# Strassen products in a conv output projection: half of two column groups as seven products of half blocks

## The chip, the cores and the metric

One core of a Trainium2 chip runs the whole program. The metric is the device time of one execution in microseconds (us). The kernel before takes 827.39 us (median of three runs, 826.68 to 827.71).

## The reference

An encoder trunk of two layers on x of 256 rows by 2048 features: a gated differential-attention layer and then a gated Conformer convolution layer, each added to x, and a final RMSNorm. The change lies at the end of the convolution layer, and in it this part matters:

```python
h = xn @ w_in + b_in                          # 2048 -> 3 x 2048
a, g, z = jnp.split(h, [CONV_WIDTH, 2 * CONV_WIDTH], axis=-1)
u = a * jax.nn.sigmoid(g)
u = depthwise_conv(u, dw, 31 taps) + dw_b     # along the rows
u = silu(layernorm(u) * ln_g + ln_b)
y = (u * jax.nn.silu(z)) @ w_out + b_out      # 256 x 2048 times 2048 x 2048
x = x + y
out = rmsnorm(x) * final_gain
```

## The kernel before, in words

All arrays are fp32. TensorE multiplies in fp32r, so each operand is held as a high part (a copy rounded to fp32r) and a low part (the operand minus its high part), and every product is three matmuls: high by high, high by low, low by high.

Weights stream through a ring of four slots (`RING`). A chunk is four k-tiles (`CK`) by 512 columns (`GW`), 1 MB. SyncE's queue loads it into `w_raw[slot]`; ScalarE makes the high part `w_hi` (`high_part`, L476) once the chunk has landed and TensorE has used the chunk four before it (`w_free`); VectorE (`low_part`, L826) or GpSimd (`low_part`, L448) makes the low part `w_lo`; TensorE multiplies; SyncE reloads the raw slot when the low part is done. Each engine works strictly through its own list, whose order is written out by hand; semaphores tie the lists together.

The convolution layer's input projection is 64 chunks (`CHUNKS_OUT` to `CHUNKS_CONV`). While TensorE works on them, VectorE makes the 30 remaining taps in PSUM (L1065) and GpSimd makes the gate products (`gate`, L461) and the low parts of chunks `POOL_FROM` up to `POOL_TO`, that is up to the fourth chunk of the output projection. Then come the layer norm (L1105 to L1112, L1118), the SiLUs, `gate_block(b)` (L1127, VectorE: silu(u) times silu(z) for two k-tiles), `block_hi(b)` (L681, ScalarE) and `block_lo(b)` (L1131, VectorE), which make the left operand of the output projection.

The output projection is 16 chunks in four column groups n = 0 to 3 of 512 columns, four chunks each; they are called chunk 0 to chunk 15 here. Each chunk is 4 k-tiles by 2 row halves (`st`) by 3 matmuls of 512 columns: 24 matmuls (`project`, L1247, L1249, L1250). Group n accumulates in banks `acc[2*(n%2)+st]`, so a group's banks have a whole further group of time to be emptied. VectorE adds b_out to the rows (`with_bias`, L1163), adds the product from PSUM (`with_product`, L1171) and multiplies by the final gain (`with_gain`, L1177). ScalarE squares the sums (L785) for the final norm. Group 3 is worked row half by row half, in banks that already hold x plus b_out, so that only half of it is left to finish at the end.

## Time and profile before

| | before |
|---|---|
| median of 3 runs | 827.39 us (826.68 to 827.71) |
| the profiled execution's own time | 826.85 us |
| span in its trace | 825.1 us |
| TensorE matmul busy | 817.6 us, 99% of the span |
| VectorE busy | 645.7 us, 78% |
| ScalarE busy | 450.1 us, 55% |
| GpSimd busy | 228.8 us, 28% |
| mean granted TensorE clock | 0.999 |

The profile is of one execution. The span goes from its first to its last instruction; 1.75 us of the execution's own time lie outside it. "Busy" of TensorE is an average that hides how tightly its matmuls follow each other: the spacing of their starts says more. PE is TensorE, DVE VectorE, ACT ScalarE, POOL GpSimd, SP SyncE.

### The profile page before, as it was taken

What the parts mean: (1) busy time and instruction counts of PE and PEld (TensorE: products, weight loads), DVE (VectorE), ACT (ScalarE), POOL (GpSimd) and SP (SyncE); (2) the same over time, 40 slices, a digit from 0 to 9 for tenths busy, and PEclk for the clock granted to TensorE, in tenths of its full rate; (3) what the DMA queues carried; (4) which work ended last, traced back from release to release, by engine and by line L of the source; (5) the groups of instructions that cost most, each with busy time, mean ns of one, the idle gap of its engine ahead of it and who ended that gap; (6) DMA issues with size and microseconds to landing.
All of it is one profiled execution on the core that took longest, in us unless ns stands there. A gap on an engine that the chain in (4) does not pass through costs nothing.

```text
span 825.1 us, 13852 instructions
## 1 busy us (share of the span) xinstructions
PE 817.6 (99%) x5628; PEld 756.1 (92%) x5628; DVE 645.7 (78%) x1099; ACT 450.1 (55%) x590; POOL 228.8 (28%) x107
## 2 busy tenths in 40 slices
PE   9999999999999999999999999999999999999996
PEld 9998899889998899888888999999999999998885
DVE  7578785697659785798788988999999998656651
ACT  7756643546436643556544465465555556694432
POOL 0300000000000000002000009988989887680000
PEclk9999999999999999999999999999999999999999
DMA  9987566536654566525655666655655565549502
GB/s 330 394 290 272 173 204 216 192 122 205 227 187 146 171 212 212 189 102 173 228 175 189 204 193 215 204 175 185 204 191 175 197 203 176 185 154 355 195 10 102
DMA packets 99809, 163.68 MB, mean 198 GB/s; under 512 B 3616, under 2 KB 40992, under 8 KB 99240
## 3 DMA queue, kind: packets, MB, share of 16 engines
q1 hardware_dynamic: 98128, 160.51, 57.8%
q10 hardware_dynamic: 1624, 2.38, 0.8%
q8 instruction: 39, 0.64, 0.3%
q14 instruction: 18, 0.15, 0.1%
HBM read 160.76 MB, written 3.69 MB: 199 GB/s over the span
## 4 chain that ended last, share of the span: by engine, by line
PE 56%; DVE 38%; ACT 4%; issue 2%; POOL 0%; ACTq 0%; DVEq 0%; POOLq 0%
DVE ps_d L1065 23%; PE ps_acc L1247 9%; PE ps_acc L1249 9%; PE ps_acc L1250 9%; PE ps_acc L1263 7%; PE ps_acc L1264 7%; PE ps_acc L1261 7%; DVE sb_w_lo L826 6%; DVE sb_zT L1017 3%; ACT sb_w_hi L476 2%; PE ps_acc L1307 1%; PE ps_acc L1311 1%; PE ps_acc L1314 1%; DVE sb_mT L980 1%; DVE sb_probs L948 1%
## 5 line engine op out<-in xcount | busy, mean ns | idle before, releaser
L476 ACT ACTIVATE sb_w_hi<-sb_w_raw 128x2048 fp32r<-128x2048 f32 x139 | 265.6, 1918 | 224.4 <-PE ps_acc L1264 151.9
L448 POOL TENSOR_TENSOR sb_w_lo<-sb_w_raw,sb_w_hi 128x2048 fp32r<-128x2048 f32 x45 | 208.2, 4633 | 389.2 <-ACT sb_w_hi L476 389.2
L826 DVE TENSOR_TENSOR sb_w_lo<-sb_w_raw,sb_w_hi 128x2048 fp32r<-128x2048 f32 x94 | 213.6, 2289 | 90.8 <-ACT sb_w_hi L476 90.4
L1261 PE MATMUL ps_acc<-sb_conv_hi,sb_w_hi 128*128 128x256 f32 x768 | 213.1, 278 | 0.0
L1264 PE MATMUL ps_acc<-sb_conv_hi,sb_w_lo 128*128 128x256 f32 x768 | 212.1, 276 | 0.0
L1263 PE MATMUL ps_acc<-sb_conv_lo,sb_w_hi 128*128 128x256 f32 x768 | 212.1, 276 | 0.0
L1065 DVE SCALAR_TENSOR_TENSOR ps_d<-sb_uT,sb_dwT,ps_d 128x256 f32<-128x256 f32 x480 | 189.0, 490 | 4.5 <-ACT ps_d L707 4.5
L1247 PE MATMUL ps_acc<-sb_w_hi,sb_act_hi 128*128 128x512 f32 x384 | 149.7, 390 | 0.0
L1249 PE MATMUL ps_acc<-sb_w_lo,sb_act_hi 128*128 128x512 f32 x384 | 149.6, 390 | 0.0
L1250 PE MATMUL ps_acc<-sb_w_hi,sb_act_lo 128*128 128x512 f32 x384 | 149.4, 389 | 0.0
L1263 PEld LDWEIGHTS ps_acc<-sb_conv_lo,sb_w_hi 128*128 128x128 f32 x768 | 144.2, 188 | 0.1
L1261 PEld LDWEIGHTS ps_acc<-sb_conv_hi,sb_w_hi 128*128 128x128 f32 x768 | 144.2, 188 | 0.1
L1264 PEld LDWEIGHTS ps_acc<-sb_conv_hi,sb_w_lo 128*128 128x128 f32 x768 | 144.2, 188 | 0.0
L1261 PE MATMUL ps_acc<-sb_act_hi,sb_w_hi 128*128 128x256 f32 x448 | 123.9, 276 | 0.0
L1264 PE MATMUL ps_acc<-sb_act_hi,sb_w_lo 128*128 128x256 f32 x448 | 123.7, 276 | 0.0
L1263 PE MATMUL ps_acc<-sb_act_lo,sb_w_hi 128*128 128x256 f32 x448 | 123.7, 276 | 0.0
L1250 PEld LDWEIGHTS ps_acc<-sb_w_hi,sb_act_lo 128*128 128x128 f32 x384 | 72.1, 188 | 15.1
L1247 PEld LDWEIGHTS ps_acc<-sb_w_hi,sb_act_hi 128*128 128x128 f32 x384 | 72.1, 188 | 15.0 <-DVE sb_act_lo L999 0.4
L1249 PEld LDWEIGHTS ps_acc<-sb_w_lo,sb_act_hi 128*128 128x128 f32 x384 | 72.1, 188 | 14.2
L1261 PEld LDWEIGHTS ps_acc<-sb_act_hi,sb_w_hi 128*128 128x128 f32 x448 | 84.1, 188 | 0.1
L1263 PEld LDWEIGHTS ps_acc<-sb_act_lo,sb_w_hi 128*128 128x128 f32 x448 | 84.1, 188 | 0.1
L1264 PEld LDWEIGHTS ps_acc<-sb_act_hi,sb_w_lo 128*128 128x128 f32 x448 | 84.1, 188 | 0.0
(171 smaller groups left out, 880.4 us busy)
## 6 DMA issues: line engine op xcount, KB each, us to landing
sb_w_raw<-in_attn_w_in SPq DMA_DIRECT2D x59, 1024.0 KB, 5.8
sb_w_raw<-in_conv_w_in SPq DMA_DIRECT2D x64, 512.0 KB, 4.6
sb_w_raw<-in_attn_w_out SPq DMA_DIRECT2D x16, 1024.0 KB, 5.0
sb_w_raw<-in_conv_w_in SPq DMA_DIRECT2D x16, 1024.0 KB, 5.1
sb_w_raw<-in_conv_w_out SPq DMA_DIRECT2D x16, 1024.0 KB, 5.0
sb_w_raw<-in_attn_w_in SPq DMA_DIRECT2D x15, 256.0 KB, 4.2
sb_xs<-in_x SPq DMA_DIRECT2D x2, 1024.0 KB, 12.3
sb_x_in<-in_x_turned SPq DMA_DIRECT2D x15, 128.0 KB, 4.0
```

The costliest lines, as they stand in the source:

```text
L448: pool.tensor_tensor(w_part(w_lo, c), w_raw[c % RING][:], w_part(w_hi, c).bitcast(F32), ALU.subtract).then_inc(lo_ready_pool, 1)
L476: act.activation(w_part(w_hi, c if like is None else like), w_raw[slot][:], ACT.Copy).then_inc(hi_ready, 1)
L826: dve.tensor_tensor(w_part(w_lo, like), w_raw[slot][:], w_part(w_hi, like).bitcast(F32), ALU.subtract).then_inc(lo_ready, 1)
L948: ins = dve.transpose(probs_turned[b * Q:(b + 1) * Q, :, :, a * Q:(a + 1) * Q], src[:, b])
L1017: ins = dve.transpose(dst, src)
L1065: dve.scalar_tensor_tensor(out_, uT[:, k, tap:tap + SEQ], dwT[:, k, tap:tap + 1], out_, ALU.mult, ALU.add).then_inc(tap_done, 1)
L1247: pe.matmul(into, left_hi, high[:, k], start=(kt == 0 and not filled), stop=False, skip_group_check=filled)
L1249: pe.matmul(into, left_hi, low[:, k], start=False, stop=False, skip_group_check=filled)
L1250: ins = pe.matmul(into, left_lo, high[:, k], start=False, stop=(kt == KT - 1), skip_group_check=filled)
L1261: pe.matmul(into, left_hi, hi[:, kt], start=(kt == 0 and f % 2 == 0), stop=False, skip_group_check=True)
L1263: pe.matmul(into, left_hi, lo[:, kt], start=False, stop=False, skip_group_check=True)
L1264: ins = pe.matmul(into, left_lo, hi[:, kt], start=False, stop=(kt == KT - 1), skip_group_check=True)
```

## The change

Chunks 0 to 3 (group 0) stay, in `acc` banks 0 and 1. Groups 1 and 2 are now interleaved: chunks 4 and 5 are their first 512 rows of weights, chunks 6 and 7 the next 512. They run one row half at a time, in four banks (`OWN_BANKS`) which ScalarE fills beforehand with x plus b_out (`fill`): group 1 has banks 3 and 0, group 2 banks 2 and 1. Banks 0 and 1 are those of group 0. Chunks 8 to 11 are the other 1024 rows of groups 1 and 2; two chunks at a time (a "quarter", q) they form a 2 by 2 matrix of half blocks (2 k-tiles by 512 columns), and with the two row halves of the left operand this is a product of 2 by 2 block matrices. It is done in Winograd's form of Strassen's scheme: seven products instead of eight, each 2 k-tiles by 3 matmuls. The sums of the left blocks (`row_sums`) and of the weight blocks (`sum_of_blocks`) are VectorE's, high and low parts are made of the sums (`sum_high`, `factor_hi` on ScalarE; `sum_low`, `factor_lo` on VectorE), and VectorE combines the products. Chunks 12 to 15 are group 3 as before.

b_out is loaded early and GpSimd adds it to all of x in two instructions of 128 x 2048, in the input projection's groups 1 and 3. GpSimd's last low part is now that of chunk 1; those of chunks 2 and 3 are VectorE's. The products of gate_block 4 to 7 go to SBUF. The diff at its core (declarations, semaphores and the renamed helpers of `project` are left out, and empty lines too):

```diff
+SEVEN_AT = CHUNKS_CONV + 2 * NCH
+SEVEN_UPTO = SEVEN_AT + NCH
+QUARTERS = 2
+FIRST = NCH - QUARTERS
+B11, B21, T3, B22, T2, T4, T1 = range(7)
+FACTORS = (B11, B21, T3, B22, T2, T4, T1)
+S1, S2, S3, S4 = range(4)
 POOL_FROM = CHUNKS_OUT + 2 * RING
-POOL_TO = CHUNKS_CONV + RING
+POOL_TO = CHUNKS_CONV + 2
...
+        def raw_factor(q, f):
+            c = SEVEN_AT + 2 * q + (f in (T3, B22, T1))
+            rows = HALVES[f in (B21, B22, T4)]
+            return w_raw[c % RING][:, rows]
...
+        def factors_done(q, f):
+            return len(FACTORS) * q + f + 1
...
+        SEVEN_BANKS = {B11: bank_a[1][:], B21: acc[:, 3], T3: bank_a[0][:], B22: acc[:, 2], T2: bank_d[0][:],
+                       T4: acc[:, 0], T1: bank_d[1][:]}
+        OWN_BANKS = {(1, 0): acc[:, 3], (2, 0): acc[:, 2], (1, 1): acc[:, 0], (2, 1): acc[:, 1]}
+        FILLED = ((1, 0), (2, 0), (1, 1), (2, 1))
+        LAST_BANKS = (bank_a[1][:], acc[:, 3])
...
+                if g == 0:
+                    sp.wait_ge(ss_ready, ST + 2 * PAIRS)
+                    sp.dma_start(b_out_bc, bass.AP(conv_b_out.tensor, conv_b_out.offset, [[0, P], [1, D]])
+                                 ).then_inc(b_out_landed, 16)
+            while c < CHUNKS:
+                n, i = conv_out_chunk(c)
+                if of_seven(c - RING):
+                    sp.wait_ge(seven_lo, len(FACTORS) * ((c - RING - SEVEN_AT) // 2 + 1))
+                else:
                     low_part_ready(sp, c - RING)
-                    load(i, cw_out[:, i * CK:(i + 1) * CK, n * GW:(n + 1) * GW])
...
+                load(c % RING, cw_out[:, i * CK:(i + 1) * CK, n * GW:(n + 1) * GW])
+                c += 1
+                if c == SEVEN_UPTO:
+                    sp.wait_ge(sum_lo, 4)
+                    sp.dma_start(gain_bc, bass.AP(final_gain.tensor, final_gain.offset, [[0, P], [1, D]])
                                  ).then_inc(final_landed, 16)
...
+                if (n, f) == (1, 0):
+                    pool.wait_ge(b_out_landed, 16)
+                    pool.wait_ge(x1_turned, PAIRS)
+                if f == 0 and n in (1, 3):
+                    st = n // 2
+                    pool.tensor_tensor(xs[:, st], xs[:, st], b_out_bc, ALU.add).then_inc(biased, 1)
                 low_part(c)
...
+                    act.wait_ge(factor_ready, 4 * q + 1 + (T3, T2, T4, T1).index(f))
+                if q:
+                    act.wait_ge(seven_used, factors_done(q - 1, f))
+                else:
+                    act.wait_ge(w_free, SEVEN_AT + f // 2 + 1)
+                act.activation(factor(w_hi, f), raw_factor(q, f), ACT.Copy).then_inc(seven_hi, 1)
+            def fill(bank, n, st):
...
+                act.activation(bank, xs[:, st, n * GW:(n + 1) * GW], ACT.Copy).then_inc(bank_filled, 1)
...
+            def sum_high(i):
+                act.wait_ge(sum_ready, 4)
+                act.activation(sums_hi[:, i].rearrange("p (q k) s -> p q k s", k=2), sums_in_place()[i], ACT.Copy
+                               ).then_inc(sum_hi, 1)
             hi_of(CHUNKS_CONV + RING)
+            act.wait_ge(acc_free, scaled_by(N_CONV - 1))
+            act.wait_ge(biased, ST)
+            fill(OWN_BANKS[1, 0], 1, 0)
+            fill(OWN_BANKS[2, 0], 2, 0)
             load_table(ACT.Sqrt)
+            for i in (S3, S4, S2, S1):
+                sum_high(i)
...
+            def last_high(i):
+                act.wait_ge(landed[i], 16 * loads_of(SEVEN_UPTO + i))
+                act.wait_ge(seven_used, factors_done(QUARTERS - 1, min(2 * i + 1, T1)))
+                act.activation(w_part(w_hi, SEVEN_UPTO + i), w_raw[i][:], ACT.Copy).then_inc(hi_ready, 1)
+            hi_of(CHUNKS_CONV + RING + 1)
+            hi_of(CHUNKS_CONV + RING + 2)
+            for st in range(ST):
+                act.wait_ge(y_ready, st + 1)
+                fill(OWN_BANKS[1 + st, 1], 1 + st, 1)
+            hi_of(CHUNKS_CONV + RING + 3)
+            act.wait_ge(sum_lo, 4)
+            for st in range(ST):
+                squares_of_y(0, st)
+            for q in range(QUARTERS):
+                for f in FACTORS:
+                    factor_hi(q, f)
+            act.wait_ge(seven_used, factors_done(QUARTERS - 1, B11))
+            act.activation(partial[:, 0], SEVEN_BANKS[B11], ACT.Copy).then_inc(first_copied, 1)
+            act.wait_ge(first_copied, 1)
+            fill(LAST_BANKS[0], PAIRS - 1, 0)
+            last_high(0)
+            act.wait_ge(y_ready, 3)
+            fill(LAST_BANKS[1], PAIRS - 1, 1)
+            for i in range(1, NCH):
+                last_high(i)
+            for n in (1, 2):
+                for st in range(ST):
+                    squares_of_y(n, st)
...
+                dve.tensor_tensor(gated_tile(b), gated_bank(b), block_of(zT, b), ALU.mult).then_inc(gated, 1)
...
+            low_part(CHUNKS_CONV + 2, 2)
             block_lo(6)
             block_lo(7)
...
+            low_part(CHUNKS_CONV + 3, 3)
...
+            def factor_lo(q, f):
+                dve.wait_ge(seven_hi, factors_done(q, f))
+                dve.tensor_tensor(factor(w_lo, f), raw_factor(q, f), factor(w_hi, f).bitcast(F32), ALU.subtract
+                                  ).then_inc(seven_lo, 1)
...
+            def row_sums():
+                s = sums_in_place()
+                a11, a12, a21, a22 = s[S2], s[S4], s[S3], s[S1]
+                dve.tensor_tensor(s[S1], a21, a22, ALU.add).then_inc(sum_ready, 1)
+                dve.wait_ge(sum_ready, 1)
+                dve.tensor_tensor(s[S3], a11, a21, ALU.subtract).then_inc(sum_ready, 1)
+                dve.wait_ge(sum_ready, 2)
+                dve.tensor_tensor(s[S2], s[S1], a11, ALU.subtract).then_inc(sum_ready, 1)
+                dve.wait_ge(sum_ready, 3)
+                dve.tensor_tensor(s[S4], a12, s[S2], ALU.subtract).then_inc(sum_ready, 1)
...
+            def sum_low(n, i):
+                dve.wait_ge(sum_hi, n + 1)
+                dve.tensor_tensor(sums_lo[:, i].rearrange("p (q k) s -> p q k s", k=2), sums_in_place()[i],
+                                  sums_hi[:, i].rearrange("p (q k) s -> p q k s", k=2).bitcast(F32), ALU.subtract
+                                  ).then_inc(sum_lo, 1)
...
+            def sum_of_blocks(q, f):
+                b11, b21, b12, b22 = (raw_factor(q, g) for g in (B11, B21, T3, B22))
+                if f == T3:
+                    for c in (SEVEN_AT + 2 * q, SEVEN_AT + 2 * q + 1):
+                        dve.wait_ge(landed[c % RING], 16 * loads_of(c))
+                    dve.tensor_tensor(b12, b22, b12, ALU.subtract).then_inc(factor_ready, 1)
+                elif f == T2:
+                    dve.wait_ge(factor_ready, 4 * q + 1)
+                    dve.wait_ge(seven_lo, factors_done(q, B11))
+                    dve.tensor_tensor(b11, b12, b11, ALU.add).then_inc(factor_ready, 1)
+                elif f == T4:
+                    dve.wait_ge(factor_ready, 4 * q + 2)
+                    dve.wait_ge(seven_lo, factors_done(q, B21))
+                    dve.tensor_tensor(b21, b21, b11, ALU.subtract).then_inc(factor_ready, 1)
+                else:
+                    dve.wait_ge(seven_lo, factors_done(q, T3))
+                    dve.tensor_tensor(b12, b22, b11, ALU.subtract).then_inc(factor_ready, 1)
...
-            low_parts(0, 4)
-            dve.wait_ge(final_landed, 32)
-            for n in range(last):
-                for st in range(ST):
-                    with_bias(n, st, xs[:, st, n * GW:(n + 1) * GW])
-                if n == 0:
-                    with_product(0)
-            low_parts(4, 6)
+            low_part(CHUNKS_CONV + RING, 0)
+            dve.wait_ge(s_lo, BLOCKS)
+            row_sums()
+            low_part(CHUNKS_CONV + RING + 1, 1)
+            for n, i in enumerate((S3, S4, S2, S1)):
+                sum_low(n, i)
+            low_part(CHUNKS_CONV + RING + 2, 2)
+            dve.wait_ge(w_free, RING + CHUNKS_CONV + NCH)
+            dve.wait_ge(biased, ST)
+            for st in range(ST):
+                dve.tensor_tensor(y_of(0, st), acc[:, st], y_of(0, st), ALU.add).then_inc(y_ready, 1)
+            low_part(CHUNKS_CONV + RING + 3, 3)
+            sum_of_blocks(0, T3)
+            factor_lo(0, B11)
+            factor_lo(0, B21)
+            sum_of_blocks(0, T2)
+            sum_of_blocks(0, T4)
+            dve.wait_ge(final_landed, 16)
             with_gain(0)
...
+            factor_lo(0, T3)
+            factor_lo(0, B22)
+            sum_of_blocks(0, T1)
+            sum_of_blocks(1, T3)
+            factor_lo(0, T2)
+            factor_lo(0, T4)
+            factor_lo(0, T1)
+            factor_lo(1, B11)
+            factor_lo(1, B21)
+            sum_of_blocks(1, T2)
+            sum_of_blocks(1, T4)
+            factor_lo(1, T3)
+            factor_lo(1, B22)
+            sum_of_blocks(1, T1)
+            factor_lo(1, T2)
+            factor_lo(1, T4)
+            factor_lo(1, T1)
+            done = factors_done(QUARTERS - 1, 0)
+            dve.wait_ge(first_copied, 1)
+            dve.wait_ge(seven_used, done + B21)
+            dve.tensor_tensor(y_of(1, 0), partial[:, 0], SEVEN_BANKS[B21], ALU.add).then_inc(y_ready, 1)
+            last_low(0)
+            dve.wait_ge(seven_used, done + T2)
+            link(dve.tensor_tensor(partial[:, 0], partial[:, 0], SEVEN_BANKS[T2], ALU.add))
+            link(dve.tensor_tensor(partial[:, 1], partial[:, 0], SEVEN_BANKS[T3], ALU.add))
+            dve.wait_ge(seven_used, done + T4)
+            dve.tensor_tensor(y_of(1, 1), partial[:, 1], SEVEN_BANKS[T4], ALU.add).then_inc(y_ready, 1)
+            last_low(1)
+            last_low(2)
+            last_low(3)
+            dve.wait_ge(seven_used, done + T1)
+            link(dve.tensor_tensor(partial[:, 0], partial[:, 0], SEVEN_BANKS[T1], ALU.add))
+            dve.tensor_tensor(y_of(2, 0), partial[:, 0], SEVEN_BANKS[B22], ALU.add).then_inc(y_ready, 1)
+            dve.wait_ge(y_ready, 4)
+            link(dve.tensor_tensor(partial[:, 1], partial[:, 1], SEVEN_BANKS[T1], ALU.add))
+            dve.tensor_tensor(y_of(2, 1), partial[:, 1], OWN_BANKS[2, 1], ALU.add).then_inc(y_ready, 1)
             with_gain(1)
...
+            for i in range(NCH):
+                c = CHUNKS_CONV + i
                 low_part_ready(pe, c)
-                if i < NCH:
-                    pe.wait_ge(s_lo, 2 * i + 1)
-                if i % NCH == 0:
-                    if n < 2:
-                        pe.wait_ge(acc_free, 2 * (G_CONV_IN + N_CONV + n + 1))
-                    else:
-                        pe.wait_ge(y_ready, 2 * (n - 1))
-                project(c, i % NCH, n % 2, conv_hi, conv_lo,
-                        (lambda: pe.wait_ge(s_lo, 2 * i + 2)) if i < NCH else None)
-            pe.wait_ge(y_ready_pre, 2 * PAIRS)
+                pe.wait_ge(s_lo, 2 * i + 1)
+                if i == 0:
+                    pe.wait_ge(acc_free, scaled_by(N_CONV - 2))
+                project(c, i, 0, conv_hi, conv_lo, lambda: pe.wait_ge(s_lo, 2 * i + 2))
...
+            for c in range(CHUNKS_CONV + NCH, SEVEN_AT):
+                n, i = conv_out_chunk(c)
+                low_part_ready(pe, c)
+                for st in range(ST):
+                    if i == 0:
+                        pe.wait_ge(bank_filled, FILLED.index((n, st)) + 1)
+                    project(c, i, 0, conv_hi, conv_lo, tiles=(st,), done=w_free if st else None,
+                            filled={st: OWN_BANKS[n, st]})
+            for q in range(QUARTERS):
+                for f in FACTORS:
+                    pe.wait_ge(seven_lo, factors_done(q, f))
+                    if q == 0:
+                        pe.wait_ge(gated, BLOCKS)
+                        if f in (T3, B22, T2, T1):
+                            pe.wait_ge(sum_lo, (T3, B22, T2, T1).index(f) + 1)
+                    into, high, low = SEVEN_BANKS[f], factor(w_hi, f), factor(w_lo, f)
+                    on = f in (B21, B22, T4)
+                    for k in range(2):
+                        left_hi, left_lo = left_tiles(q, f, k)
+                        end = q == QUARTERS - 1 and k == 1
+                        pe.matmul(into, left_hi, high[:, k], start=(q == 0 and k == 0 and not on), stop=False,
+                                  skip_group_check=on)
+                        pe.matmul(into, left_hi, low[:, k], start=False, stop=False, skip_group_check=on)
+                        ins = pe.matmul(into, left_lo, high[:, k], start=False, stop=end, skip_group_check=on)
+                    ins.then_inc(seven_used, 1)
             for st in range(ST):
+                pe.wait_ge(bank_filled, len(FILLED) + st + 1)
                 for i in range(NCH):
                     if st == 0:
                         low_part_ready(pe, CHUNKS - NCH + i)
                     project(CHUNKS - NCH + i, i, (PAIRS - 1) % 2, conv_hi, conv_lo, tiles=(st,),
-                            done=rows_done if i == NCH - 1 else None, filled=True)
```

## Rows read from the trace of the kernel before

**Rows 1.** The page: busy us, share of the span and instructions.
```profile
PE 817.6 (99%) x5628; PEld 756.1 (92%) x5628; DVE 645.7 (78%) x1099; ACT 450.1 (55%) x590; POOL 228.8 (28%) x107
```
**Rows 2.** Waits, TensorE's only one: us in total, times, longest us.
```profile
PE ps_d L1364 <- POOL sb_ones L426: 1.0, 1, 1.0
```
**Rows 3.** Timeline of TensorE, output projection: start us, us, instruction.
```profile
731.47 0.40 PE L1247 MATMUL ps_acc<-sb_w_hi,sb_conv_hi 128*128 128x512 f32 x1
...
753.26 0.39 PE L1247 MATMUL ps_acc<-sb_w_hi,sb_conv_hi 128*128 128x512 f32 x1
...
755.98 0.39 PE L1247 MATMUL ps_acc<-sb_w_hi,sb_conv_hi 128*128 128x512 f32 x1
...
818.31 0.39 PE L1250 MATMUL ps_acc<-sb_w_hi,sb_conv_lo 128*128 128x512 f32 x1
```
**Rows 4.** Timeline of VectorE, 737 to 803 us; idle before it in brackets.
```profile
738.33 0.70 DVE L1127 TENSOR_TENSOR ps_d<-ps_d,sb_zT 128x512 f32<-128x512 f32 x1
738.94 0.68 DVE L1131 TENSOR_TENSOR sb_conv_lo<-ps_a,sb_conv_hi 128x512 fp32r<-128x512 f32 x1
...
755.47 2.29 DVE L826 TENSOR_TENSOR sb_w_lo<-sb_w_raw,sb_w_hi 128x2048 fp32r<-128x2048 f32 x1 [3.15 <-ACT sb_w_hi L476]
757.68 1.29 DVE L1163 TENSOR_TENSOR sb_xs<-sb_xs,sb_b_out_bc 128x512 f32<-128x512 f32 x2
758.88 1.28 DVE L1171 TENSOR_TENSOR sb_xs<-ps_acc,sb_xs 128x512 f32<-128x512 f32 x2
```
**Rows 5.** Timeline of VectorE, a dependent pair and its successor.
```profile
704.46 0.69 DVE L1118 TENSOR_TENSOR sb_uT<-sb_uT,ps_d 128x512 f32<-128x512 f32 x1 [2.19 <-PE ps_d L1403]
705.18 0.69 DVE L1120 TENSOR_TENSOR sb_uT<-sb_uT,ps_d 128x512 f32<-128x512 f32 x1
```
**Rows 6.** Timeline of ScalarE, 722 to 761 us.
```profile
722.84 0.57 ACT L681 ACTIVATE sb_conv_hi<-ps_a 128x512 fp32r<-128x512 f32 x1
723.31 0.58 ACT L681 ACTIVATE sb_conv_hi<-ps_d 128x512 fp32r<-128x512 f32 x1
...
739.56 1.92 ACT L476 ACTIVATE sb_w_hi<-sb_w_raw 128x2048 fp32r<-128x2048 f32 x1
741.49 1.28 ACT L481 ACT_TABLE_LOAD   x1
742.79 0.20 ACT L481 ACTIVATE sb_small<-sb_small 128x1 f32<-128x1 f32 x1
742.90 1.91 ACT L476 ACTIVATE sb_w_hi<-sb_w_raw 128x2048 fp32r<-128x2048 f32 x1
748.08 1.92 ACT L476 ACTIVATE sb_w_hi<-sb_w_raw 128x2048 fp32r<-128x2048 f32 x1 [3.27 <-PE ps_acc L1250]
753.52 1.92 ACT L476 ACTIVATE sb_w_hi<-sb_w_raw 128x2048 fp32r<-128x2048 f32 x1 [3.52 <-PE ps_acc L1250]
```
**Rows 7.** Timeline of GpSimd: a gate, two low parts, and the last four.
```profile
537.36 1.47 POOL L461 TENSOR_TENSOR sb_uT<-sb_a_rows,sb_uT 128x256 f32<-128x256 f32 x2
...
544.15 4.63 POOL L448 TENSOR_TENSOR sb_w_lo<-sb_w_raw,sb_w_hi 128x2048 fp32r<-128x2048 f32 x1 [0.71 <-ACT sb_w_hi L476]
549.59 4.63 POOL L448 TENSOR_TENSOR sb_w_lo<-sb_w_raw,sb_w_hi 128x2048 fp32r<-128x2048 f32 x1 [0.81 <-ACT sb_w_hi L476]
...
723.01 18.41 POOL L448 TENSOR_TENSOR sb_w_lo<-sb_w_raw,sb_w_hi 128x2048 fp32r<-128x2048 f32 x4 [6.40 <-ACT sb_w_hi L476]
```
**Rows 8.** DMA issues: what, queue, count, KB each, median us to landing.
```profile
sb_w_raw<-in_conv_w_out SPq DMA_DIRECT2D x16, 1024.0 KB, 5.0
...
sb_gain_bc<-in_final_gain SPq DMA_DIRECT2D x1, 1024.0 KB, 8.9
```
**Rows 9.** Timeline of ScalarE in the input projection's first group.
```profile
470.02 0.62 ACT L642 ACTIVATE sb_squared<-sb_xs 128x512 f32<-128x512 f32 x1
...
480.90 5.52 ACT L476 ACTIVATE sb_w_hi<-sb_w_raw 128x2048 fp32r<-128x2048 f32 x3
```
**Rows 10.** Windows after TensorE's last matmul: busy us, then PEclk, DMA share, GB/s.
```profile
822.30:822.80 0.50, 0.00 (x0) 0.00 (x0) 0.00 (x0) 0.00 (x0) 0.00 (x0) 1.00 1.01 381
822.80:823.30 0.50, 0.00 (x0) 0.00 (x0) 0.00 (x0) 0.00 (x0) 0.00 (x0) 0.57 1.01 389
823.30:823.80 0.50, 0.00 (x0) 0.00 (x0) 0.00 (x0) 0.00 (x0) 0.00 (x0) 0.50 1.01 373
```
**Rows 11.** Timeline of TensorE at the program's start.
```profile
1.00 4.21 PE L1364 MATMUL ps_d<-sb_ones 128*128 128x128 f32 x18 [1.00 <-POOL sb_ones L426]
4.86 1.20 PE L1307 MATMUL ps_acc<-sb_act_hi,sb_w_hi 128*128 128x256 f32 x4
...
7.36 0.63 PE L1307 MATMUL ps_acc<-sb_act_hi,sb_w_hi 128*128 128x256 f32 x4
7.83 0.62 PE L1311 MATMUL ps_acc<-sb_act_lo,sb_w_hi 128*128 128x256 f32 x4
```

More of the change, by code:

```diff
@@ L161, in build @@
         with ExitStack() as one:
-            b_out_bc = sb("b_out_bc", [P, D], F32, one)
-            gain_bc = sb("gain_bc", [P, D], F32, one)
-            junk = sb("junk", [P, ST, GW], F32, one)
+            sums_hi = sb("sums_hi", [P, 4, 2 * QUARTERS, P], F32R, one)
+            sums_lo = sb("sums_lo", [P, 4, 2 * QUARTERS, P], F32R, one)
         acc = psum("acc", [P, 4, GW])
@@ L300, in by_pool, with of_seven, conv_out_chunk, factor @@
             return c == POOL_SEAM or POOL_FROM <= c < POOL_TO
+        def of_seven(c):
+            return SEVEN_AT <= c < SEVEN_UPTO
+        def conv_out_chunk(c):
+            at = (c - CHUNKS_CONV - NCH) // 2
+            if c < CHUNKS_CONV + NCH or c >= SEVEN_UPTO:
+                return (0 if c < SEVEN_AT else PAIRS - 1), c % NCH
+            return 1 + c % 2, at
+        def raw_factor(q, f):
+            c = SEVEN_AT + 2 * q + (f in (T3, B22, T1))
+            rows = HALVES[f in (B21, B22, T4)]
+            return w_raw[c % RING][:, rows]
+        def factor(parts, f):
+            at = ROWS_AT + f % 2 * 2 * GW
+            return parts[f // 2][:, at:at + 2 * GW].rearrange("p (k n) -> p k n", k=2)
+        def factors_done(q, f):
+            return len(FACTORS) * q + f + 1
+        def loads_of(c):
+            doubled = min(max(c // RING + 1 - CHUNKS_OUT // RING, 0), Z_FROM)
+            return c // RING + 1 + doubled
+        SEVEN_BANKS = {B11: bank_a[1][:], B21: acc[:, 3], T3: bank_a[0][:], B22: acc[:, 2], T2: bank_d[0][:],
[3 more added lines that the diff above has]
+        LAST_BANKS = (bank_a[1][:], acc[:, 3])
+        def gated_tile(b):
+            return block_of(zT, b) if b >= 2 * FIRST else gated_bank(b)
+        def sums_in_place():
+            tiles = rows_and_tiles(zT)
+            (a11, a21), (a12, a22) = [[tiles[:, a, :, :, st * P:(st + 1) * P] for st in range(ST)] for a in range(2)]
+            return {S1: a22, S2: a11, S3: a21, S4: a12}
+        def rows_and_tiles(t):
+            return t[:, CK * FIRST:].rearrange("p (q a k) s -> p a q k s", a=2, k=2)
         def place(c, low):
@@ L317, in low_part_ready @@
         def low_part_ready(eng, c):
-            done = sum(by_pool(b) == by_pool(c) for b in range(c + 1))
+            done = sum(by_pool(b) == by_pool(c) and not of_seven(b) for b in range(c + 1))
             eng.wait_ge(lo_ready_pool if by_pool(c) else lo_ready, done)
@@ L1191, in _ @@
-            low_parts(4, 6)
-            with_gain(0)
-            low_parts(6, 7)
-            with_product(1)
-            for st in range(ST):
-                dve.wait_ge(y_ready, 2 + st + 1)
-                with_bias(last, st, acc[:, 2 * (last % 2) + st])
-            low_parts(7, 10)
+            def sum_of_blocks(q, f):
[12 more added lines that the diff above has]
+                    dve.tensor_tensor(b21, b21, b11, ALU.subtract).then_inc(factor_ready, 1)
+                else:
+                    dve.wait_ge(seven_lo, factors_done(q, T3))
+                    dve.tensor_tensor(b12, b22, b11, ALU.subtract).then_inc(factor_ready, 1)
@@ L1244, in project @@
                     for st in tiles:
-                        into = acc[:, 2 * par + st]
+                        into = filled[st] if filled else acc[:, 2 * par + st]
                         left_hi, left_lo = hi[:, kt, st * P:(st + 1) * P], lo[:, kt, st * P:(st + 1) * P]
                         pe.matmul(into, left_hi, high[:, k], start=(kt == 0 and not filled), stop=False,
-                                  skip_group_check=filled)
-                        pe.matmul(into, left_hi, low[:, k], start=False, stop=False, skip_group_check=filled)
+                                  skip_group_check=bool(filled))
+                        pe.matmul(into, left_hi, low[:, k], start=False, stop=False, skip_group_check=bool(filled))
                         ins = pe.matmul(into, left_lo, high[:, k], start=False, stop=(kt == KT - 1),
-                                        skip_group_check=filled)
+                                        skip_group_check=bool(filled))
                 if done:
@@ L1442, in _ @@
                     project(CHUNKS - NCH + i, i, (PAIRS - 1) % 2, conv_hi, conv_lo, tiles=(st,),
-                            done=rows_done if i == NCH - 1 else None, filled=True)
+                            done=rows_done if i == NCH - 1 else None, filled=LAST_BANKS)
 def kernel(**inputs):
```

77 lines of the change are left out of this document (35 added, 42 removed).

## The prediction

> **What bounds the kernel now.** I read the page's first part, the waits, then TensorE's timeline of the last stage, and after that the lists of the three other engines around it. TensorE is busy 99% of the span, VectorE 78% [rows 1], and TensorE's only recorded wait is 1.0 us at the start [rows 2]: everywhere else its next operand is there in time. In the output projection the first of 384 matmuls starts at 731.47 and the last at 818.31 [rows 3]; 86.84 us over 383 steps are 0.2267 us a matmul. A row half of a chunk (12) takes 2.72 us, a chunk (24) 5.44, a group (96) 21.77; group 0 ends when the matmul at 753.26 starts [rows 3]. So time is won only by fewer matmuls, and lost wherever TensorE is made to wait. The question is whether each new wait is met.
>
> **What is removed.** In a quarter 8 block products of 6 matmuls become 7. Two quarters: 96 become 84, 12 fewer, 12 x 0.2267 = 2.72 us. Every other matmul stays. This gain is sure, as long as the spacing holds.
>
> **The input projection.** GpSimd adds b_out twice, 128 x 2048 each, 4.63 us by its low part of that size [rows 7]. Behind them stand low parts and the gates of group 2. GpSimd sits idle 0.7 to 0.8 us per chunk of 5.44 [rows 7], so it runs up to 4.6 us late after the first add and some 5.7 after the second (between them it regains about 3 x 0.8 us a group, less 1.45 for the gates). A high part is made when TensorE frees its slot, which leaves three chunks, 16.3 us; high 1.9 plus low 4.6 leave 9.8 spare. It holds. The late gate delays a first tap on ScalarE by under 3 us, which the taps need a group later. SyncE's new wait stands ahead of the loads of the second group until the squares at 470.02 are done; with b_out ahead of them three loads come some 8 us late, near 479 for the first, but ScalarE converts them only from 480.90 [rows 9]. Cost 0; if one load came later than that, TensorE still has about 4.5 us before it needs it.
>
> **The start of the output projection.** VectorE takes over two low parts. gate_block 7 starts at 738.33 and the next instruction at 738.94 [rows 4]. From there, with 2.21 per low part (755.47 to 757.68) and 0.61 per 512 columns (738.33 to 738.94) [rows 4]: low 2 runs from 738.94 to 741.15 (TensorE wants it at 731.47 + 10.9 = 742.4: 1.2 spare), block_lo 6 and 7 to 742.37, low 3 to 744.58 (wanted 747.8), low 4 to 746.79. Now row_sums: four sums of 512 columns, each waiting for the one before, 0.72 apart [rows 5]; the last ends at 749.64. ScalarE had finished high 4, the two fills and the table by then (741.5 + 2 x 0.6 + 1.4 = 744.1 [rows 6]), but in its list high 5 stands behind the four sum_high, which wait for that last sum. At 0.48 each [rows 6] they end the wait at 751.6, and high 5 takes until 753.5 (1.92 [rows 6]). VectorE's next entry is low 5: it idles 3.9 us. Then low 5 from 753.54 to 755.75, four sum_low at 0.61 to 758.19, low 6 to 760.40 (high 6 is ready by 755.4), and only then the sum of group 0, which empties banks 0 and 1.
>
> **The wait that this meets.** TensorE ends group 0 at 753.26 and does 12 matmuls in bank 3, until 755.98 [rows 3]. The 12 after them go to bank 0. In the kernel before that bank had a whole group, 21.77 us, to be emptied, and VectorE came to it at 758.88 [rows 4], 5.6 us after the group's end, at no cost. Now it needs: sum of 0.69 from 760.40 to 761.1, ScalarE's fill of 0.6 to 761.7, TensorE on at about 761.75. That is a stall of 761.75 - 755.98 = 5.8 us, all of it on the path, as nothing later has slack of TensorE's own. Behind the waiting matmul stand all others, and behind the wait for the sum on ScalarE stands high 7, which TensorE wants only 13 us later. Bounds: VectorE's work alone from 738.94, without the idle time, is 5 x 2.21 + 2 x 0.61 + 2.85 + 4 x 0.61 = 17.6, so 756.5, and the stall 1.9: the lower end. If the sums of strided blocks cost twice their rows, 5 us come on top: 10.8. I take 5.8, since every entry has a row of its size.
>
> **Clock.** After TensorE's last matmul its granted clock stands at 1.00 until 822.8, then falls to 0.50, the 1.2 GHz level [rows 10]: 4.1 us of idleness after the last one's end (818.7). The stall of 5.8 is longer, so the clock has probably fallen when TensorE goes on. At the start of the program, matmuls run from 1.00, four of 256 columns take 1.0 us from 4.86, and from 7.36 the next four start 0.47 later [rows 11]: some 6.2 us of work at the lower level. There every matmul takes twice as long, so half of that time is lost: 0 (no fall) to 3.1 us. I take 2.0, since the stall ends soon after the fall and the start's warm-up is the longest case. The Trainium skill ("TensorE: Matmul & The Clock Gate", section "Why this matters for your kernels") speaks against this change: idle gaps between bursts of matmuls put the array back to half its clock. The end of this trace agrees (1.00 to 0.50 at 822.8).
>
> **The seven products.** TensorE would begin them at 753.26 + 21.77 + 5.8 = 780.8, and needs a factor every 1.36 us. VectorE after the sums: low 7 to 766.4, then per quarter 7 low parts and 4 sums of 1024 columns, 1.14 each (between 0.61 for 512 and 2.21 for 2048 [rows 4]): 12.5 us against TensorE's 9.5. It is the slower of the two, but has a lead: gain_bc, loaded behind chunk 11 at 766.4, lands by about 776 (8.9 [rows 8]) and holds VectorE for some 4 us; the first quarter's last factor is then ready at 784.2 (wanted 789.0), the second's at 795.2 (wanted 798.5). ScalarE's factor_hi, 1.0 each, waits for TensorE. Cost 0, with 3.3 us to spare; a fall of the clock makes it more.
>
> **The last group.** It begins at 799.9. Chunks 14 and 15 load only once the second quarter's factors are done, at 795.2; with 5.0 for a load [rows 8] and some 2.5 more for the second they land at 800.2 and 803; high and low parts make 804.3 and 807, wanted at 805.3 and 808.0. About 1 us to spare, so a cost of 0 to 1.5 if a load is slow; I take 0. The final sums and gains (four of the eight sums behind low 15) delay the first row half's norm to about 812.8, 2 us behind its matmuls, but the end hangs on the second half, 10.9 us later. The tail of 6.4 us after TensorE stays.
>
> **The sum.** Against the profiled execution's own 826.85 us (825.1 of span and 1.75 around it): -2.7 + 5.8 + 2.0 = +5.1, 831.9 us. The median shown is 0.5 above that execution, so this may come out at 832.4 as well; I state 831.9.
>
> **Rivals.** (a) The stall comes, but the clock does not fall or is back at once: 829.9. For it: one end-of-program window is all that shows the fall, and it came only 1.7 us sooner after the last matmul than the stall would last. (b) Faster, 824.1: the banks are handed over within the 2.72 us of bank 3, and the saving shows whole. It decides at VectorE starting group 0's sum by 754.7, some 5.7 us before my time. For it: only that ScalarE would have to reach high 5 before the sums, and VectorE's 17.6 us of work would have to shrink by 1.8. Against it: the lists, which are strict. (c) VectorE becomes the bound of the seven products: its 3.0 us a quarter of excess work are not covered, or the loads of chunks 14 and 15 come late. With the stall: 833 to 836. Against it: the lead of 3.3 us. (d) The low part of chunk 2 is late (1.2 spare): a small stall early, which only moves the same start of the group's sum; 832 to 833, within the range of the forecast.
>
> **How the numbers follow.** Forecast, stall and fall, 0.55 (830.5 to 834 of its own); (a) 0.28; (b) 0.08; (c) 0.06; near the old time for reasons I don't see 0.03. Range of 8 in 10: from below (a) to above the forecast with the full 3.1, 829.2 to 834.3. A difference of 0.2% is 1.65 us, about what a measurement tells from no change: faster 0.09, same 0.04, slower 0.87.
>
> **What would show it.** In the changed trace: TensorE idle near 756 for about 5.8 us, ended by ScalarE's copy into bank 0; VectorE idle near 749.7 to 753.5 before low 5, released by a high part; the granted clock at 0.5 after the gap and matmuls 0.43 to 0.46 apart for some microseconds; 84 matmuls in the seven products at 0.227 without a gap; TensorE's last matmul near 823. The prediction is wrong if there is no gap at bank 0, if VectorE reaches group 0's sum before 755, or if the gap stands in the seven products or in front of the last group.

## The result: 834.87 us, 0.9% slower

The changed kernel takes 834.87 us (median of 6 runs, 834.1 to 835.59) against 827.57 us in the same runs for the kernel before (826.68 to 828.19): ratio 1.0088, 95% interval 1.0075 to 1.0101, +7.3 us. The profiled execution took 835.41 us, its span is 833.6. The direction and the main mechanism were forecast, but the time lies 0.6 us above the range. Starts, waits and gaps below are those of profiled executions.

Who made TensorE wait, in the changed kernel (us in total, times, longest); it answers to [rows 2], where one line stood:

```profile
PE ps_acc L1458 <- ACT ps_acc L870: 5.8, 1, 5.8
PE ps_a L1434 <- ACT sb_uT L794: 1.4, 1, 1.4
PE ps_d L1575 <- POOL sb_ones L497: 1.0, 1, 1.0
PE ps_a L1568 <- issue: 0.6, 1, 0.6
PE ps_a L1458 <- DVE sb_w_lo L1323: 0.5, 1, 0.5
PE ps_acc L1472 <- DVE sb_w_lo L957: 0.3, 1, 0.3
```

L870 is the fill of a bank, L794 the copy of the taps' result before the layer norm, L1323 a low part of the last group. The gap at bank 0, from TensorE's timeline (answers to [rows 3]):

```profile
758.41 0.39 PE L1461 MATMUL ps_acc<-sb_w_hi,sb_conv_lo 128*128 128x512 f32 x1
764.59 0.79 PE L1458 MATMUL ps_acc<-sb_w_hi,sb_conv_hi 128*128 128x512 f32 x1 [5.79 <-ACT ps_acc L870]
...
767.74 0.44 PE L1460 MATMUL ps_acc<-sb_w_lo,sb_conv_hi 128*128 128x512 f32 x1
```

6.18 us from start to start, 5.95 more than the usual 0.23. The seven matmul steps after it (from one start to the next) take 3.15 us where 1.59 are usual: 1.56 lost to the clock. The windows around it (busy us of PE, PEld, DVE, ACT, POOL, then the granted clock) show the level; they answer to [rows 10]:

```profile
758.40:764.60 6.20, 0.41 (x3) 0.01 (x1) 6.10 (x8) 0.66 (x2) 0.00 (x0) 0.71 0.52 174
764.60:768.00 3.40, 3.40 (x8) 2.69 (x9) 1.00 (x1) 3.40 (x5) 0.00 (x0) 0.53 0.81 300
768.00:771.00 3.00, 3.00 (x14) 2.44 (x13) 3.00 (x3) 1.99 (x4) 0.00 (x0) 1.00 0.12 32
```

Finer windows of the gap itself show when the clock fell: 2.2 us after the last matmul before the gap had ended, at 758.80.

```profile
758.90:761.00 2.10, 0.00 (x0) 0.00 (x0) 2.10 (x4) 0.00 (x0) 0.00 (x0) 1.00 0.46 116
761.00:764.50 3.50, 0.00 (x0) 0.00 (x0) 3.50 (x4) 0.56 (x1) 0.00 (x0) 0.50 0.62 235
```

What VectorE and ScalarE did before that fill (answers to [rows 4 to 6]); first VectorE, then ScalarE:

```profile
741.05 0.69 DVE L1258 TENSOR_TENSOR sb_zT<-ps_d,sb_zT 128x512 f32<-128x512 f32 x1
...
751.64 0.69 DVE L1311 TENSOR_TENSOR sb_zT<-sb_zT 128x512 f32<-128x512 f32 x1
756.40 2.29 DVE L957 TENSOR_TENSOR sb_w_lo<-sb_w_raw,sb_w_hi 128x2048 fp32r<-128x2048 f32 x1 [4.07 <-ACT sb_w_hi L553]
758.61 2.49 DVE L1316 TENSOR_TENSOR sb_sums_lo<-sb_zT,sb_sums_hi 128x512 fp32r<-128x512 f32 x4
761.02 2.28 DVE L957 TENSOR_TENSOR sb_w_lo<-sb_w_raw,sb_w_hi 128x2048 fp32r<-128x2048 f32 x1
763.22 1.28 DVE L1366 TENSOR_TENSOR sb_xs<-ps_acc,sb_xs 128x512 f32<-128x512 f32 x2
```

```profile
752.37 2.19 ACT L875 ACTIVATE sb_sums_hi<-sb_zT 128x512 fp32r<-128x512 f32 x4 [5.62 <-DVE sb_zT L1311]
754.47 3.71 ACT L553 ACTIVATE sb_w_hi<-sb_w_raw 128x2048 fp32r<-128x2048 f32 x2
763.94 1.20 ACT L870 ACTIVATE ps_acc<-sb_xs 128x512 f32<-128x512 f32 x2 [5.76 <-DVE sb_xs L1366]
```

VectorE's last left-block sum, the 4.07 us of waiting for high 5, and group 0's sum 22.2 us after gate_block 7 (forecast: 22.1) are there.

Two things in the trace are not as forecast. The whole stage stands 2.7 us later than before: gate_block 7 starts at 741.05, before at 738.33 [rows 4]. And gaps of 0.9 us in all stand in the last group, the larger behind the load of chunk 15. ScalarE in the input projection's second group (answers to [rows 9]), and in the last group:

```profile
484.09 1.92 ACT L553 ACTIVATE sb_w_hi<-sb_w_raw 128x2048 fp32r<-128x2048 f32 x1 [0.26 <-DMA sb_w_raw<-in_conv_w_in]
487.10 1.92 ACT L553 ACTIVATE sb_w_hi<-sb_w_raw 128x2048 fp32r<-128x2048 f32 x1 [1.08 <-DMA sb_w_raw<-in_conv_w_in]
490.12 1.92 ACT L553 ACTIVATE sb_w_hi<-sb_w_raw 128x2048 fp32r<-128x2048 f32 x1 [0.83 <-DMA sb_w_raw<-in_conv_w_in]
...
804.84 1.93 ACT L899 ACTIVATE sb_w_hi<-sb_w_raw 128x2048 fp32r<-128x2048 f32 x1 [1.97 <-DMA sb_w_raw<-in_conv_w_out]
809.02 1.93 ACT L899 ACTIVATE sb_w_hi<-sb_w_raw 128x2048 fp32r<-128x2048 f32 x1 [2.25 <-DMA sb_w_raw<-in_conv_w_out]
```

Before, the first three of the second group's high parts ran back to back from 480.90 to 486.42 and the fourth began at 487.48. Here the first starts at 481.93 without a wait, and the other three each wait for their load. The delay reaches the taps through a chain over three engines. VectorE's fourth low part ends later; behind it in VectorE's list stand the scalings of the first group (L1070 before, L1201 now); ScalarE's sigmoids need them, GpSimd's gate needs the sigmoids, ScalarE's first tap (L782) the gate, and VectorE's taps the first tap. VectorE waits the same 4.53 us for that first tap in both kernels, so all of the delay is older than this wait. The first lines are the kernel before, the last two the changed one:

```profile
491.65 0.68 DVE L1070 TENSOR_TENSOR sb_a_rows<-ps_acc,sb_rstd_conv 128x512 f32<-128x512 f32 x1
497.47 5.97 DVE L1065 SCALAR_TENSOR_TENSOR ps_d<-sb_uT,sb_dwT,ps_d 128x256 f32<-128x256 f32 x15 [4.53 <-ACT ps_d L707]
...
494.28 0.68 DVE L1201 TENSOR_TENSOR sb_a_rows<-ps_acc,sb_rstd_conv 128x512 f32<-128x512 f32 x1
500.09 1.28 DVE L1196 SCALAR_TENSOR_TENSOR ps_d<-sb_uT,sb_dwT,ps_d 128x256 f32<-128x256 f32 x3 [4.53 <-ACT ps_d L782]
```

1.0 of these 2.6 us is older: in this execution TensorE reached a point of the attention layer at 92.20 instead of 91.17 (the wait called "issue" above). The profiled executions of the kernels below reached it between 90.7 and 91.7, so it differs from execution to execution. The other 1.6 us come from the loads, and come back as TensorE's wait of 1.4 for the taps' last copy.

Why the loads came late can be read from SyncE's list. In the kernel before, the first of the second group's loads goes out at 462.19; in the changed one SyncE stands at its new wait until 471.78, issues b_out (into `squared`, the space of the squares, which is why it must wait for them), and only then the weights. The first line is the kernel before:

```profile
462.19 0.92 SPq L345 DMA_DIRECT2D sb_w_raw<-in_conv_w_in  x2
...
471.78 0.34 SPq L470 DMA_DIRECT2D sb_squared<-in_conv_b_out  x1
472.17 2.42 SPq L410 DMA_DIRECT2D sb_w_raw<-in_conv_w_in  x4
459.00:471.70 12.70, 12.70 (x83) 11.52 (x82) 12.55 (x17) 6.60 (x11) 1.00 (x2) 1.00 0.00 0
480.00:500.00 20.00, 20.00 (x177) 19.95 (x176) 12.68 (x15) 14.38 (x15) 2.30 (x3) 1.00 1.09 344
```

The last two lines are windows of the changed kernel: nothing is moved from 459.0 to 471.7 (0 GB/s, last figure), and from 480 to 500 the transfers follow one another at 344 GB/s, at which 1 MB takes 3.0 us.

The account without the 1.0 us of the attention layer: -2.72 (12 matmuls) + 5.95 (gap) + 1.6 (clock) + 1.6 (late taps) + 0.9 (last group) = +7.3, which is the difference of the medians. That it fits to a tenth is partly luck: in other executions the clock's term is up to 2.5 (experiments 2 and 8), the late taps cost 1.2 to 1.6, and the last group's gap is not always there. The profiled execution has the other 1.0 too: 8.3 of its 8.56.

### The profile page after: what moved, and what is told of

It is laid out like the page before. It is cut to its first block, busy times and chain, and to the rows that moved or that the text cites. A ratio compares the mean times of both kernels' runs of the same rounds, so it can differ in the third digit from the quotient of the medians.

```text
span 833.6 us, 13900 instructions
## 1 busy us (share of the span) xinstructions
PE 817.6 (98%) x5616; PEld 754.4 (91%) x5616; DVE 669.2 (80%) x1123; ACT 463.1 (56%) x611; POOL 228.3 (27%) x107
## 4 chain that ended last, share of the span: by engine, by line
PE 42%; DVE 41%; ACT 8%; DMA 4%; issue 3%; SPq 1%; ACTq 0%; DVEq 0%
DVE ps_d L1196 22%; PE ps_acc L1458 7%; PE ps_acc L1460 7%; PE ps_acc L1461 7%; DVE sb_w_lo L957 6%; PE ps_acc L1472 6%; PE ps_acc L1474 6%; PE ps_acc L1475 6%; DVE sb_zT L1148 3%; ACT sb_w_hi L553 3%; DMA sb_xs<-in_x 2%; DMA sb_w_raw<-in_conv_w_out 1%; DMA sb_w_raw<-in_conv_w_in 1%; DVE sb_mT L1111 1%; DVE sb_probs L1079 1%
## 5 line engine op out<-in xcount | busy, mean ns | idle before, releaser
L553 ACT ACTIVATE sb_w_hi<-sb_w_raw 128x2048 fp32r<-128x2048 f32 x131 | 250.1, 1917 | 180.2 <-PE ps_acc L1475 133.4
L519 POOL TENSOR_TENSOR sb_w_lo<-sb_w_raw,sb_w_hi 128x2048 fp32r<-128x2048 f32 x43 | 198.4, 4628 | 381.3 <-ACT sb_w_hi L553 381.3
L957 DVE TENSOR_TENSOR sb_w_lo<-sb_w_raw,sb_w_hi 128x2048 fp32r<-128x2048 f32 x88 | 199.9, 2289 | 80.0 <-ACT sb_w_hi L553 79.6
```

The lines of the kernel that those rows point to most:

```text
L519: pool.tensor_tensor(w_part(w_lo, c), w_raw[c % RING][:], w_part(w_hi, c).bitcast(F32), ALU.subtract).then_inc(lo_ready_pool, 1)
L553: act.activation(w_part(w_hi, c if like is None else like), w_raw[slot][:], ACT.Copy).then_inc(hi_ready, 1)
L957: dve.tensor_tensor(w_part(w_lo, like), w_raw[slot][:], w_part(w_hi, like).bitcast(F32), ALU.subtract).then_inc(lo_ready, 1)
```

## The experiments

All times of experiments are medians; each ratio, with its 95% interval, is to the kernel before, run on the same chip. Experiments 1 to 4 ran on one chip (kernel before: 827.02 us), 5 to 8 on another (827.36), and the changed kernel's 834.87 stands beside 827.57. Differences across these sets, to the changed kernel above all, are therefore known only to some 0.6 us; those within a set, and the traces, are firmer.

**1. ScalarE's order.** Theory: VectorE's list in front of group 0's sum makes the gap.

```diff
-            for i in (S3, S4, S2, S1):
-                sum_high(i)
...
             hi_of(CHUNKS_CONV + RING + 1)
             hi_of(CHUNKS_CONV + RING + 2)
+            for i in (S3, S4, S2, S1):
+                sum_high(i)
```

> The changed kernel, with ScalarE's high parts of chunks 5 and 6 put ahead of the four sum_high in its list; nothing else. Theory (the stall at bank 0 is VectorE's list, made longer by the 4.1 us for which it waits for high 5): VectorE no longer idles before low 5, reaches group 0's sum about 4 us sooner, TensorE's gap of 6.2 us falls to about 2, the clock does not fall any more (1.6 us), and the time is 5.5 to 6 us under the changed kernel's, near 829.2. Rival (the gap is ScalarE's fill or TensorE's own wait, and VectorE's idle time costs nothing): gap and time stay, 834.9.

Measured: 828.94 us, 1.0020 (1.0011 to 1.0030). The gap is 2.01 us from start to start, and the clock stays up:

```profile
758.93 0.50 PE L1458 MATMUL ps_acc<-sb_w_hi,sb_conv_hi 128*128 128x512 f32 x1 [1.62 <-ACT ps_acc L870]
```

VectorE goes from the last block sum to low 5 without a pause:

```profile
750.14 0.69 DVE L1311 TENSOR_TENSOR sb_zT<-sb_zT 128x512 f32<-128x512 f32 x1
750.75 2.28 DVE L957 TENSOR_TENSOR sb_w_lo<-sb_w_raw,sb_w_hi 128x2048 fp32r<-128x2048 f32 x1
752.96 2.49 DVE L1316 TENSOR_TENSOR sb_sums_lo<-sb_zT,sb_sums_hi 128x512 fp32r<-128x512 f32 x4
755.36 2.28 DVE L957 TENSOR_TENSOR sb_w_lo<-sb_w_raw,sb_w_hi 128x2048 fp32r<-128x2048 f32 x1
757.57 1.28 DVE L1366 TENSOR_TENSOR sb_xs<-ps_acc,sb_xs 128x512 f32<-128x512 f32 x2
```

Two lines in the order of a list cost 5.9 us by the two medians (5.4 with each kernel against the kernel before of its own runs). The remaining gap (1.8 over the usual) is the lower end that the prediction worked out, 1.9.

**2. b_out later.**

```diff
-                if g == 0:
+                if g == 2:
                     sp.wait_ge(ss_ready, ST + 2 * PAIRS)
                     sp.dma_start(b_out_bc, ...)
...
-                if (n, f) == (1, 0):
+                if (n, f) == (3, 0):
                     pool.wait_ge(b_out_landed, 16)
-                if f == 0 and n in (1, 3):
-                    st = n // 2
+                if f == 0 and n in (3, 5):
+                    st = n // 5
```

> The changed kernel, with the load of b_out issued behind the loads of the input projection's third group instead of its first, and GpSimd's two adds in groups 3 and 5 instead of 1 and 3. Theory (b_out's load, with SyncE's wait in front of it, made the next chunks' high and low parts late, so that VectorE began the taps 1.6 us later, and it never makes this up): TensorE's wait of 1.4 us for the last copy before the layer norm goes, VectorE begins the taps as early as before, and the time is 1.6 us under the changed kernel's, near 833.3. Rival (the lateness comes from GpSimd's adds, which hold up the gates): it stays, since the adds are still made beside the taps, 834.9.

Measured: 833.5 us (4 runs), 1.0071 (1.0054 to 1.0088), 1.4 under the changed kernel (0.8 with each against the kernel before of its own runs). The taps begin at 497.44, as before the change, and the wait for L794 is gone:

```profile
497.44 5.97 DVE L1196 SCALAR_TENSOR_TENSOR ps_d<-sb_uT,sb_dwT,ps_d 128x256 f32<-128x256 f32 x15 [4.53 <-ACT ps_d L782]
```

The interval overlaps that of the changed kernel (1.0075 to 1.0101), so the trace carries this one, not the time. The same edit is timed again in experiment 6, against experiment 5 on the same chip: 1.35 us.

**3. TensorE kept at work in the gap.**

```diff
                     if i == 0:
+                        for _ in range(24 if (n, st) == (1, 1) else 0):
+                            pe.matmul(bank_d[0][:], conv_hi[:, 0, 0:P], w_part(w_hi, c)[:, 0], start=True, stop=True)
                         pe.wait_ge(bank_filled, FILLED.index((n, st)) + 1)
```

> The changed kernel, with 24 matmuls of 512 columns into an unused bank put where TensorE waits for bank 0 (5.4 of the 6.0 us); their result is not read. Theory (the idle stretch lets the granted clock fall, and 8 matmuls of 0.43 instead of 0.23 us follow): the clock stays at its upper level, the stall stays, and the time is 1.5 us under the changed kernel's, near 833.4. Rival (the slow matmuls come from the operands' being late or are made up later): no difference, 834.9.

Measured: 832.27 us, 1.0059 (1.0042 to 1.0076), 2.6 under the changed kernel (2.0 with each against the kernel before of its own runs) where 1.5 were expected. The stall is as long as it was: from 757.85, where the first added matmul starts, to the first real one at 763.80 are 5.95 us. In the windows this stretch and what follows are at the upper level:

```profile
757.80:763.80 6.00, 5.66 (x26) 4.34 (x25) 5.91 (x8) 0.66 (x2) 0.00 (x0) 1.00 0.59 178
763.80:768.00 4.20, 4.20 (x18) 3.47 (x19) 1.79 (x1) 4.20 (x7) 0.00 (x0) 1.00 0.66 249
```

The slow matmuls are gone, so the clock is the cause of them. That it is more than 1.5 has likely two reasons. First, the slow matmuls do not always cost the same: in the profiled executions of experiments 2 and 8, which have the same gap, they cost 2.5 and 2.4 us (12 and 11 steps) instead of 1.56 (7). There the clock fell later in the gap, 4.1 and 3.8 us after the last matmul's end instead of 2.2, and rose later, 5.2 and 4.8 us after the first matmul instead of 3.2. Second, the profiled execution here has hardly a gap in the last group. The load of chunk 15, issued 0.4 us behind that of chunk 14, landed 7.3 us after its issue here, and 8.5 to 8.8 in the changed kernel and in experiments 1, 2, 4, 5 and 8. Why it was in time isn't settled.

**4. Both orders.** ScalarE as in 1, and on VectorE:

```diff
             low_part(CHUNKS_CONV + RING + 1, 1)
-            for n, i in enumerate((S3, S4, S2, S1)):
-                sum_low(n, i)
-            low_part(CHUNKS_CONV + RING + 2, 2)
             dve.wait_ge(w_free, RING + CHUNKS_CONV + NCH)
             dve.wait_ge(biased, ST)
             for st in range(ST):
                 dve.tensor_tensor(y_of(0, st), acc[:, st], y_of(0, st), ALU.add).then_inc(y_ready, 1)
+            for n, i in enumerate((S3, S4, S2, S1)):
+                sum_low(n, i)
+            low_part(CHUNKS_CONV + RING + 2, 2)
```

> The changed kernel, with ScalarE's order of the first experiment and on VectorE the sum of group 0 put ahead of the four sum_low and low 6. Theory: bank 0 is emptied and filled by about 2 us after group 0's end, within the 2.7 us of matmuls in bank 3; no gap and no fall of the clock, 7.5 us under the changed kernel's time, near 827.4, equal to the kernel before; what is left against the full gain of 2.7 us is the late start of the taps (1.6) and the gap in the last group (0.8). Rival (the seven products then lack the lead that the stall gave VectorE, and its 12.5 us a quarter against TensorE's 9.5 decide): a new gap of 2 to 3 us in the products, 830.

Measured: 828.66 us, 1.0018 (1.0008 to 1.0027), where 827.4 was expected: the gap at bank 0 is gone, yet the time is that of experiment 1. TensorE's waits on the last group's low parts have grown from 0.5 to 2.5 us:

```profile
PE ps_a L1458 <- DVE sb_w_lo L1323: 2.5, 3, 1.2
```

VectorE decides now, as the rival said, but a step later than it said: the products run without a gap, the last group has three (1.08, 1.57 and 0.97 us from start to start, of which 0.23 each are usual). VectorE's wait for the final gain in the middle of its list shows where its lead went:

```profile
772.27 1.29 DVE L1334 TENSOR_TENSOR sb_xs<-sb_xs,sb_zT 128x512 f32<-128x512 f32 x2 [3.72 <-DMA sb_zT<-in_final_gain]
```

**5. The gain's product later.** On top of experiment 4:

```diff
             sum_of_blocks(0, T4)
-            dve.wait_ge(final_landed, 16)
-            with_gain(0)
...
+            dve.wait_ge(final_landed, 16)
+            with_gain(0)
             with_gain(1)
             with_gain(2)
```

> The fourth experiment's kernel (both orders), with VectorE's product of group 0 with the final gain moved behind the seven products, to the other two groups' gains. Theory (without the stall VectorE decides in the last group, and 3.7 us of its list went into waiting for the final gain's load and 1.2 into the product): the three gaps of 2.9 us in all in the last group go, 2.5 to 3 us under the fourth experiment's 828.7, near 826. Rival (the gaps come from the loads of chunks 14 and 15, which wait for the last factors whatever VectorE does before): the gaps stay within 1 us, 828.

Measured: 826.43 us, 0.9987 (0.9977 to 0.9997), 2.2 less than experiment 4 (2.6 with each against the kernel before of its own chip). Two of the three gaps are gone, as the theory said. One of 0.9 us is left (0.7 over the usual), as the rival said: it is chunk 15's, whose load landed 8.8 us after its issue.

**6. And b_out later: the version that beats both.** Experiments 5 and 2 together.

> The fifth experiment's kernel, with b_out loaded and added later as in the second. Theory: its 1.4 us come on top, since both are on the path one after the other: near 824.5, and against the kernel before the whole 2.7 us of the seven products, a ratio of 0.997. Rival (what the taps lose is made up before the output projection): no further gain, 826.

Measured: 825.08 us (7 runs), 0.9971 (0.9960 to 0.9982): 0.3% faster than the kernel before. In the profiled execution TensorE's list of waits is again one line, and its matmuls leave no gap over 0.34 us in the output projection:

```profile
PE ps_d L1575 <- POOL sb_ones L497: 1.0, 1, 1.0
```

That execution is one of the fast ones, 823.84 us: it reached the point of the attention layer at 90.69, 0.5 us sooner than the kernel before, and chunk 15's load landed 7.4 us after its issue. No edit of this version touches that load, so the last gap may well be there in other executions of it; no trace shows that.

**7. The gain taken back.** Experiment 6 with as many matmuls as the scheme saves:

```diff
                     on = f in (B21, B22, T4)
+                    for _ in range(12 if (q, f) == (0, T1) else 0):
+                        pe.matmul(into, conv_hi[:, 0, 0:P], high[:, 0], start=True, stop=True)
```

> The sixth experiment's kernel with 12 matmuls of 512 columns added among the seven products (as many as the scheme saves; their result is not used). Theory (TensorE's count of matmuls is what the time follows once the waits are gone): 12 x 0.2267 = 2.7 us more than the sixth experiment's time, 827.2, the time of the kernel before. Rival (the other engines bound the products, and 12 matmuls fit into waiting): under 1 us more.

Measured: 827.21 us, 0.9998 (0.9989 to 1.0008): 2.1 more than 6 by the medians, 2.7 by the spans of the profiled executions (824.7 and 822.0). The seven products are worth what was worked out, once nothing waits.

**8. Without GpSimd's adds.**

```diff
-                    pool.tensor_tensor(xs[:, st], xs[:, st], b_out_bc, ALU.add).then_inc(biased, 1)
+                    pool.memset(grants[:, 6:7], 0.0).then_inc(biased, 1)
```

> The changed kernel with GpSimd's two adds of b_out left out (a tiny write in their place; b_out is not in the sum), its load as in the changed kernel. Theory (the load of b_out delays the taps, not the adds): VectorE's first tap and TensorE's wait of 1.0 to 1.4 us before the layer norm stay, the time stays at 834.9. Rival (the adds hold up the gates): the wait goes and the time falls by 1.5 us.

Measured: 834.81 us (2 runs), 1.0090 (1.0071 to 1.0108), as the changed kernel. The high parts wait for their loads as there, and so does the end of the taps:

```profile
486.04 1.92 ACT L553 ACTIVATE sb_w_hi<-sb_w_raw 128x2048 fp32r<-128x2048 f32 x1 [1.09 <-DMA sb_w_raw<-in_conv_w_in]
489.03 1.92 ACT L553 ACTIVATE sb_w_hi<-sb_w_raw 128x2048 fp32r<-128x2048 f32 x1 [0.81 <-DMA sb_w_raw<-in_conv_w_in]
```

```profile
PE ps_a L1434 <- ACT sb_uT L794: 1.4, 1, 1.4
```

The adds cost nothing; b_out's load, with the wait ahead of it, is what delays the taps. The two were not taken apart by a run, but SyncE's lines above give an estimate. Without b_out's own 3.0 us the second group's last three loads would have landed near 481, 484 and 487, before ScalarE wanted them (482.7, 484.5 and 487.5 in the kernel before, 1.0 later in this execution). Without the wait, b_out would have had the idle time from 459 on to itself. So it likely took both.

## Why the prediction was right in kind and wrong in size

Two terms that the prediction put at nothing failed, the input projection's above all; the others held.

- The saving, "12 x 0.2267 = 2.72 us": right; 2.1 to 2.7 by experiments 6 and 7.
- The stall at bank 0, 5.8: measured 5.95, by the very entries named, with the idle time before low 5 at 4.07 (3.9). Experiments 1 and 4 show it to be the order of two lists.
- The clock, 2.0 from a range of 0 to 3.1: it fell, and cost 1.56 in the profiled execution, 2.4 and 2.5 in those of experiments 8 and 2. The 4.1 us of idleness that the prediction took from the end of the trace were the late end of what was seen: 2.2, 3.8 and 4.1.
- The input projection, "Cost 0": the step that failed; it cost 1.6. The prediction let b_out's load make three loads late, "near 479 for the first", with ScalarE converting "only from 480.90", and then gave TensorE's own slack of 4.5 us as the cover. It asked about the first load only, and that one did land in time (at 481.0, converted at 481.93). The three behind it landed 3.0 us apart, so that the high parts, which take 1.8 each when nothing holds them, came one load apart and the fourth 1.6 us late (490.12 for 487.48, less the 1.0 of the attention layer). TensorE's slack did cover that. But behind these parts stand the scalings, gates and first tap that VectorE's taps wait for, and from the taps to the layer norm VectorE has no slack (busy for all of the 198.7 us from 500.2 to 698.9): what it loses at the start TensorE pays at the end (L794). The cost was asked of TensorE alone, and it was on a second chain, visible in the page's chain that ended last (23% of the span on VectorE's L1065, more than on any other line), which the prediction did not use.
- The seven products, 0: right; TensorE did the 84 without a gap.
- The last group, "a cost of 0 to 1.5 if a load is slow; I take 0": 0.9. The mechanism was named; the term that was mis-sized is "some 2.5 more for the second" load, which no row showed. It was 3.8 more (8.8 us after its issue, against 5.0 for the first), and in three of nine profiled executions it was 2.3, which is in time.
- The base: the forecast was added to the profiled execution's 826.85, while the kernel before has a median of 827.57 in the runs that count. This is 0.7 of the 3.0 us by which the forecast was short; the two missing terms are 2.5, and the clock gave 0.4 back.
- The range: its upper end lies 2.4 above the forecast, of which 1.1 are the clock's (3.1 for 2.0) and 1.3 belong to no term. The two missing terms, 1.6 and 0.9, are together 2.5. With them the forecast's own sum is 834.4.
- The slower rival (c), 833 to 836, holds the measured time, and the half of it that has the load late came true (chunk 15's, 0.9). But most of the excess over the forecast is the late taps, which no rival named; and the other half, VectorE as the bound, showed only once the stall was gone (experiment 4).
- The faster rival, 824.1, is what experiment 6 is nearest to, and it took four edits.
